# Two layer stacks on one core: resident tensors at 2048-byte addresses, feed-forward row sums ahead of the weights' low parts

## The chip, the core and the metric

The kernel runs on one core of a Trainium2 chip. A core has five engines: TensorE (PE in the profile; its weight loads are PEld), VectorE (DVE), ScalarE (ACT), GpSimd (POOL) and SyncE (SP), which issues the DMAs here. The metric is device time in microseconds. Before the change the median of three runs is 2491.5 us (2491.39 to 2491.71).

## The reference

A residual stream x of 512 tokens x 1024 features goes through two layers of a first stack and two layers of a second one, all in float32.

```
for l in range(2):                                  # first stack
    hn = rms_norm(h, g_mix[l]); q, k, v, xr, gr = split(hn @ w_in[l])
    o = differential attention(rope(q), rope(k), v); y = rg_lru(conv(xr)) * gelu(gr)
    h = h + concat(o, y) @ w_out[l]
    hm = rms_norm(h, g_mlp[l])
    h = h + square(relu(hm @ w_mlp_in[l])) @ w_mlp_out[l]
    h = h + sigmoid(rms_norm(h, g_ple[l]) @ w_ple_gate[l]) * (p[l] @ w_ple_proj[l])
x = rms_norm(h, g_final)
for l in range(2):                                  # second stack
    u, q, k, v, iq, ik, iw = split(rms_norm(x, g_pre_mix[l]) @ w_in[l])
    mix = concat(pool_mixer(u), attention(q, k, v over the top 128 keys by iq, ik, iw)) @ w_out[l]
    x = x + rms_norm(mix, g_post_mix[l])
    f = square(relu(rms_norm(x, g_pre_ffn[l]) @ w_ff1[l])) @ w_ff2[l]
    x = x + rms_norm(f, g_post_ffn[l])
```

The feed-forward width is 4096, in four blocks of 1024.

## The kernel before

Everything is kept transposed: features on the 128 partitions, the 512 tokens along the row. A float32 product is made of three passes in the fp32r format: each operand is split into a rounded high part and the low part that is left, and TensorE adds high x high, high x low and low x high (`three_passes`, its matmul is L472). The weights stream through SBUF in chunks of 128 x 2048 floats. SP loads a chunk into one half of `wr`; ScalarE rounds it into `wh` (L406) and VectorE subtracts to get `wl` (L412); TensorE reads `wh` and `wl` as the stationary operand (128 columns at a time). The moving operand is the normed stream in `gh`/`gl` or the hidden values in `hh`/`hl`. The names change places in every second stage: in stages 2 and 4 of the four the stream is in `hh`/`hl` and the hidden values in `gh`/`gl`. In the second stack a few first chunks are put where the hidden values will be, and so `gh` or `hh` is the stationary operand there.

A feed-forward layer has four blocks. In each, 4 chunks (8 tiles of 24 matmuls of 512 columns) make the hidden values, and 4 chunks add their product with the second matrix. In the first three blocks ("fast" blocks, 12 in the kernel) this second product has seven half-width products in the place of eight: GpSimd forms sums of the weights (`sum_weights`, L752 to L757), ScalarE and VectorE split each of the seven forms (L769, L781), and the hidden values need sums too. Those are made pair by pair of tiles: `rectify` (L703) takes a tile out of PSUM, ScalarE squares it (L789, L790), `even_low` (L809, L810), `other_sums` (L818 to L821), `odd_low` (L828) and `sums_low` (L835, L838) give the sums and their low parts, the last from what ScalarE rounds in L796 and L802. The matmuls of that second product have 256 columns; those on `rounded` read the sums.

Nothing is scheduled by a planner. Each engine's program is written out in order, engines are in step by semaphores, and an instruction that waits holds all that stands behind it on its engine. `fast_block_dve` is VectorE's order for a fast block. Before the even tile of pair i = 3 is through `even_low`, TensorE cannot start the fourth part of the first form; before L838 of pair 3 it cannot end the forms two to five. In the second stack VectorE waits, ahead of the first fast block, until GpSimd has zeroed the rows to which the result is added (`zeroed`, L2070).

Of the kernel before, what the change touches and what calls it, by code (L numbers as in the profile page):

```python
# [138 lines left out]
def build(nc, weights, params_a, params_b, gains, gates, embed, constants, positions, xt, out):  # L139

    with ExitStack() as ctx:
        def sb(name, shape, dtype=F32):
            return ctx.enter_context(nc.sbuf_tensor(name, shape, dtype))


        tiles = {name: sb(name, [P, KT, S], F32R) for name in ("gh", "gl", "hh", "hl")}
        with nc.sbuf_tensor("rounded", [P, ARENA], F32R) as rounded:
            pass
        arena = sb("arena", [P, ARENA])
        rest = dict(  # L150
            x=sb("x", [P, KT, S]), wr=sb("wr", [P, 2, CHUNK]), wh=sb("wh", [P, 2, CHUNK], F32R), wl=sb("wl", [P, 2, CHUNK], F32R),
            cst=sb("cst", [P, C_N]), par=sb("par", [P, max(AP_N, BP_N)]), rb=sb("rb", [P, S]), sq=sb("sq", [P, 2, S]),
            tmp=sb("tmp", [P, 4, S]), small=sb("small", [P, 256]), extra=sb("extra", [P, 7 * HALF + 2 * S]), rounded=rounded, arena=arena,
            ps=ctx.enter_context(nc.psum_tensor("ps", [P, 8, S], F32)))
# [669 lines left out]
def odd_low(dve, mem, sem, p):  # L824

    k = 2 * (p % PAIRS) + 1
    dve.wait_ge(sem["hidden_high"], 4 * p + 4)
    dve.tensor_tensor(mem.hl[:, k, :], mem.tmp[:, 3, :], mem.hh[:, k, :].bitcast(F32), ALU.subtract).then_inc(sem["hidden_low"], 1)  # L828


def sums_low(dve, mem, sem, p):

    q = p % PAIRS
    dve.wait_ge(sem["sums_high"], 2 * p + 1)
    dve.tensor_tensor(mem.hl[:, 2 * q, HALF:S], mem.tmp[:, 2, 0:HALF], mem.hh[:, 2 * q, HALF:S].bitcast(F32), ALU.subtract)  # L835
# [136 lines left out]
def fast_block_dve(dve, mem, sem, c0, j, tile_of, split_ahead, bank, target):  # L972

    for i in range(BC):
        p = PAIRS * j + i
        rectify(dve, mem, sem, tile_of[c0 + i], 2 * i, bank=bank(tile_of[c0 + i]))
        even_low(dve, mem, sem, p)
        rectify(dve, mem, sem, tile_of[c0 + i] + 1, 2 * i + 1, bank=bank(tile_of[c0 + i] + 1))
        if i < 2 and split_ahead:
            split_low(dve, mem, sem, c0 + i + 2)  # L980
        if i == 2:
            form_low(dve, mem, sem, c0 + BC, range(4))
        other_sums(dve, mem, sem, p)
# [929 lines left out]
def second_stack_layer(stage, layer, weights, params, gains, positions, out):  # L1913
# [301 lines left out]
    def program_dve(dve):  # L2215
# [650 lines left out]
```

## Time and profile before

| what | value |
|---|---|
| median of three runs | 2491.5 us |
| the profiled execution's own time | 2496.87 us |
| its span, first to last instruction | 2495.1 us |
| PE busy | 2395.5 us, 96% |
| DVE busy | 1737.2 us, 70% |
| ACT busy | 1062.2 us, 43% |
| POOL busy | 796.8 us, 32% |
| mean granted TensorE clock | 0.985 |

The span and the execution's own time are 1.8 us apart. TensorE is busy nearly all the time; matmuls are pipelined, so one's duration in a row (0.39 us) is longer than the distance from start to start (0.23 us), and it is this distance that counts. A clock of 1.00 in a window is 2.4 GHz, 0.50 is 1.2 GHz.

### The profile page before, as it was taken

What the parts mean: (1) busy time and instruction counts of PE and PEld (TensorE: products, weight loads), DVE (VectorE), ACT (ScalarE), POOL (GpSimd) and SP (SyncE); (2) the same over time, 40 slices, a digit from 0 to 9 for tenths busy, and PEclk for the clock granted to TensorE, in tenths of its full rate; (3) what the DMA queues carried; (4) which work ended last, traced back from release to release, by engine and by line L of the source; (5) the groups of instructions that cost most, each with busy time, mean ns of one, the idle gap of its engine ahead of it and who ended that gap; (6) DMA issues with size and microseconds to landing.
All of it is one profiled execution on the core that took longest, in us unless ns stands there. A gap on an engine that the chain in (4) does not pass through costs nothing.

```text
span 2495.1 us, 34122 instructions
## 1 busy us (share of the span) xinstructions
PE 2395.5 (96%) x13186; PEld 1984.8 (80%) x13186; DVE 1737.2 (70%) x2881; ACT 1062.2 (43%) x1739; POOL 796.8 (32%) x606
## 2 busy tenths in 40 slices
PE   8999999999999999999999998999999999899997
PEld 6876888988787788898876876988886777788886
DVE  6786777845778577784569857786657966777753
ACT  4554434434355443443432453444343245434431
POOL 2002344501200243450247522352312832254412
PEclk9999999999999999999999999999999999899999
DMA  4211123132231212323222120322321211132231
GB/s 155 97 65 68 68 101 119 68 118 85 100 103 59 72 68 101 119 76 111 85 89 85 55 86 34 108 79 102 119 102 56 85 51 69 51 119 98 72 119 51
DMA packets 33230, 216.23 MB, mean 87 GB/s; under 512 B 4144, under 2 KB 4400, under 8 KB 8112
## 3 DMA queue, kind: packets, MB, share of 16 engines
q1 hardware_dynamic: 33072, 214.08, 24.3%
q8 instruction: 105, 1.72, 0.3%
q14 instruction: 53, 0.43, 0.1%
HBM read 211.97 MB, written 2.10 MB: 86 GB/s over the span
## 4 chain that ended last, share of the span: by engine, by line
PE 54%; DVE 14%; issue 13%; POOL 11%; ACT 5%; DMA 3%; SPq 0%; POOLq 0%; ACTq 0%; DVEq 0%
PE ps L472 47%; DVE wl L412 4%; DMA wr<-in_weights 3%; POOL arena L752 2%; ACT wh L406 2%; DVE wl L781 2%; POOL arena L754 2%; POOL arena L945 2%; POOL arena L757 1%; POOL arena L756 1%; POOL x L945 1%; DVE tmp L703 1%; PE ps L2622 1%; PE ps L2577 1%; DVE gl L694 1%
## 5 line engine op out<-in xcount | busy, mean ns | idle before, releaser
L472 PE MATMUL ps<-gh,wh 128*128 128x512 f32 (+2 forms) x1480 | 555.1, 375 | 33.9 <-DVE gl L694 10.3
L472 PE MATMUL ps<-hh,wh 128*128 128x512 f32 (+2 forms) x1448 | 540.6, 373 | 24.7 <-DVE hl L809 9.5
L472 PE MATMUL ps<-gl,wh 128*128 128x512 f32 (+2 forms) x1480 | 544.3, 368 | 0.0
L472 PE MATMUL ps<-gh,wl 128*128 128x512 f32 (+2 forms) x1480 | 543.9, 368 | 0.0
L472 PE MATMUL ps<-hh,wl 128*128 128x512 f32 (+2 forms) x1448 | 530.5, 366 | 0.0
L472 PE MATMUL ps<-hl,wh 128*128 128x512 f32 (+2 forms) x1448 | 530.4, 366 | 0.0
L412 DVE TENSOR_TENSOR wl<-wr,wh 128x2048 fp32r<-128x2048 f32 x120 | 278.5, 2321 | 197.1 <-ACT wh L406 194.9
L472 PEld LDWEIGHTS ps<-gh,wh 128*128 128x128 f32 (+1 forms) x1480 | 281.1, 190 | 99.7 <-issue 18.3
L406 ACT ACTIVATE wh<-wr 128x2048 fp32r<-128x2048 f32 x136 | 259.5, 1909 | 211.4 <-PE ps L472 125.8
L472 PEld LDWEIGHTS ps<-hh,wh 128*128 128x128 f32 (+1 forms) x1448 | 274.1, 189 | 87.2 <-issue 21.3
L472 PEld LDWEIGHTS ps<-gh,wl 128*128 128x128 f32 (+1 forms) x1480 | 281.1, 190 | 50.8
L472 PEld LDWEIGHTS ps<-gl,wh 128*128 128x128 f32 (+1 forms) x1480 | 280.7, 190 | 48.7 <-issue 1.4
L472 PEld LDWEIGHTS ps<-hh,wl 128*128 128x128 f32 (+1 forms) x1448 | 274.5, 190 | 48.9
L472 PEld LDWEIGHTS ps<-hl,wh 128*128 128x128 f32 (+1 forms) x1448 | 274.0, 189 | 47.3 <-issue 1.4
L472 PE MATMUL ps<-rounded,wh 128*128 128x256 f32 x1152 | 212.8, 283 | 4.6 <-DVE rounded L838 3.3
L781 DVE TENSOR_TENSOR wl<-arena,wh 128x512 fp32r<-128x512 f32 x192 | 179.4, 960 | 10.3 <-ACT wh L769 10.3
L769 ACT ACTIVATE wh<-arena 128x512 fp32r<-128x512 f32 x192 | 112.6, 625 | 171.0 <-POOL arena L754 86.3
L472 PEld LDWEIGHTS ps<-rounded,wh 128*128 128x128 f32 x1152 | 177.9, 191 | 7.1 <-DVE rounded L838 4.9
L472 PE MATMUL ps<-rounded,wl 128*128 128x256 f32 x576 | 162.3, 282 | 0.0
L703 DVE SCALAR_TENSOR_TENSOR tmp<-ps,rb 128x512 f32<-128x512 f32 x128 | 87.6, 686 | 99.1 <-PE ps L472 81.0
L781 DVE TENSOR_TENSOR wl<-wr,wh 128x512 fp32r<-128x512 f32 x144 | 142.0, 994 | 20.9 <-ACT wh L769 20.9
L752 POOL TENSOR_TENSOR arena<-wr 128x512 f32<-128x512 f32 x48 | 74.1, 1544 | 235.8 <-DMA wr<-in_weights 235.8
(303 smaller groups left out, 3703.7 us busy)
## 6 DMA issues: line engine op xcount, KB each, us to landing
wr<-in_weights SPq DMA_DIRECT2D x195, 1024.0 KB, 4.7
out_yt<-x SPq DMA_DIRECT2D x8, 256.0 KB, 2.0
x<-in_xt SPq DMA_DIRECT2D x3, 512.0 KB, 8.9
wr<-in_weights SPq DMA_DIRECT2D x2, 512.0 KB, 5.8
arena<-in_gates SPq DMA_DIRECT2D x2, 512.0 KB, 8.0
arena<-in_embed SPq DMA_DIRECT2D x2, 512.0 KB, 5.6
par<-in_params_b SPq DMA_DIRECT2D x2, 274.0 KB, 2.8
x<-in_xt SPq DMA_DIRECT2D x2, 256.0 KB, 4.6
```

Source lines behind the costliest of these rows:

```text
L406: act.activation(sem.high_part(c), mem.wr[:, sem.buffer(c), :], ACT.Copy).then_inc(sem["high"], 1)
L412: dve.tensor_tensor(sem.low_part(c), mem.wr[:, sem.buffer(c), :], sem.high_part(c).bitcast(F32), ALU.subtract)\
L472: done = pe.matmul(out, stationary, moving, start=(first and n == 0), stop=(last and n == 2), skip_group_check=True)
L694: dve.scalar_tensor_tensor(out=mem.gl[:, k, :], in0=mem.x[:, k, :], scalar=gains[:, k:k + 1], in1=mem.gh[:, k, :].bitcast(F32), op0=ALU.mu ...
L703: dve.scalar_tensor_tensor(out=mem.tmp[:, k % 2, :], in0=mem.ps[:, tile % 4 if bank is None else bank, :], scalar=0.0, in1=mem.rb[:, :], o ...
L752: pool.tensor_tensor(sums[:, 0, :], raw[:, 3, :], raw[:, 2, :], ALU.add).then_inc(sem["weight_sums"], 1)
L754: pool.tensor_tensor(sums[:, 1, :], sums[:, 0, :], raw[:, 0, :], ALU.subtract).then_inc(sem["weight_sums"], 1)
L756: pool.tensor_tensor(sums[:, 2, :], raw[:, 1, :], sums[:, 1, :], ALU.subtract).then_inc(sem["weight_sums"], 1)
L757: pool.tensor_tensor(sums[:, 3, :], raw[:, 0, :], raw[:, 3, :], ALU.subtract).then_inc(sem["weight_sums"], 1)
L769: act.activation(sem.form(c, f)[0], weight_form(mem, sem, c, f), ACT.Copy) .then_inc(sem["high" if f == FORMS - 1 else "form_high"], 1)
L781: done = dve.tensor_tensor(low, weight_form(mem, sem, c, f), high.bitcast(F32), ALU.subtract)
L945: last = pool.tensor_tensor(target[row][:, part], target[row][:, part], u[:, n, :], ALU.add)
```

## The change

There are three edits.

Addresses. Tensors are laid out one after another. The first one began at 1024 + 128 = 1152 bytes of each partition, and a new tensor `margin` of 896 bytes lets it begin at 2048. `gh`, `gl`, `hh`, `hl` have 16384 bytes each, so they began at 1152 modulo 2048 and begin at 0 now. The arena has 15376 x 4 = 61504 bytes, which is 64 more than a multiple of 2048. It stood ahead of `x`, `wr`, `wh`, `wl`, so these began at 1216 modulo 2048; it now stands behind them, and they begin at 0. The arena, and `rounded` over the same bytes, began at 1152 and begin at 0 too. `cst`, `par`, `rb`, `sq`, `tmp`, `small` and `extra` come behind all of these in both kernels; `cst` began at 1216 and begins at 64.

VectorE's order in a fast block. `sums_low` is cut in two, and `first_sum_low`, `other_sums` and `odd_low` go ahead of the split of the next weights. In the first pair of a block, in the first stack (L412 is the split of a chunk, L703 the next tile), VectorE has before:

```order
L703 SCALAR_TENSOR_TENSOR tmp<-ps,rb 128x512
L412 TENSOR_TENSOR wl<-wr,wh 128x2048
L818 TENSOR_TENSOR extra<-tmp 128x256
L819 TENSOR_TENSOR extra<-tmp 128x256
L821 TENSOR_TENSOR extra<-tmp,extra 128x256
L828 TENSOR_TENSOR hl<-tmp,hh 128x512
L835 TENSOR_TENSOR hl<-tmp,hh 128x256
L838 TENSOR_TENSOR rounded<-extra,rounded 128x768
```

and now, where L824, L825, L827, L834, L841 and L849 are the old L818, L819, L821, L828, L835 and L838, L709 is L703 and L418 is L412:

```order
L709 SCALAR_TENSOR_TENSOR tmp<-ps,rb 128x512
L841 TENSOR_TENSOR hl<-tmp,hh 128x256
L824 TENSOR_TENSOR extra<-tmp 128x256
L825 TENSOR_TENSOR extra<-tmp 128x256
L827 TENSOR_TENSOR extra<-tmp,extra 128x256
L834 TENSOR_TENSOR hl<-tmp,hh 128x512
L418 TENSOR_TENSOR wl<-wr,wh 128x2048
L849 TENSOR_TENSOR rounded<-extra,rounded 128x768
```

Five instructions pass the split, and one (L835, now L841) passes four others as well. In the third pair the first four forms' lows (L781) stand where the split stood. VectorE has there before:

```order
L781 TENSOR_TENSOR wl<-wr,wh 128x512
L781 TENSOR_TENSOR wl<-arena,wh 128x512 x3
L818 TENSOR_TENSOR extra<-tmp 128x256
L819 TENSOR_TENSOR extra<-tmp 128x256
L821 TENSOR_TENSOR extra<-tmp,extra 128x256
L828 TENSOR_TENSOR hl<-tmp,hh 128x512
L835 TENSOR_TENSOR hl<-tmp,hh 128x256
```

and now, with L787 for L781:

```order
L841 TENSOR_TENSOR hl<-tmp,hh 128x256
L824 TENSOR_TENSOR extra<-tmp 128x256
L825 TENSOR_TENSOR extra<-tmp 128x256
L827 TENSOR_TENSOR extra<-tmp,extra 128x256
L834 TENSOR_TENSOR hl<-tmp,hh 128x512
L787 TENSOR_TENSOR wl<-wr,wh 128x512
L787 TENSOR_TENSOR wl<-arena,wh 128x512 x3
```

The same five pass four instructions. In the fourth pair only L835 moves. In the first fast block of a layer of the second stack pairs one and two have no split, and there, too, only L835 moves.

The wait for the zeroed rows. It stood ahead of the first `rectify` of the second stack's feed-forward layers and stands ahead of the first addition of a block now, some 45 instructions later.

```diff
@@ build
+        sb("margin", [P, (2048 - DMA_SCRATCH % 2048 - 128) // 4])
         tiles = {name: sb(name, [P, KT, S], F32R) for name in ("gh", "gl", "hh", "hl")}
-        with nc.sbuf_tensor("rounded", [P, ARENA], F32R) as rounded:
-            pass
-        arena = sb("arena", [P, ARENA])
         rest = dict(
             x=sb("x", [P, KT, S]), wr=sb("wr", [P, 2, CHUNK]), wh=sb("wh", [P, 2, CHUNK], F32R), wl=sb("wl", [P, 2, CHUNK], F32R),
+            rounded=overlaid("rounded", [P, ARENA], F32R), arena=sb("arena", [P, ARENA]),
...
-def sums_low(dve, mem, sem, p):
+def first_sum_low(dve, mem, sem, p):
     q = p % PAIRS
     dve.wait_ge(sem["sums_high"], 2 * p + 1)
     dve.tensor_tensor(mem.hl[:, 2 * q, HALF:S], ...)
+
+def other_sums_low(dve, mem, sem, p):
+    q = p % PAIRS
     dve.wait_ge(sem["sums_high"], 2 * p + 2)
     dve.wait_ge(sem["hidden_sums"], 4 * p + 3)
     dve.tensor_tensor(mem.tl[:, q, :], ...)
@@ fast_block_dve
         rectify(dve, mem, sem, tile_of[c0 + i] + 1, 2 * i + 1, bank=bank(tile_of[c0 + i] + 1))
+        first_sum_low(dve, mem, sem, p)
+        other_sums(dve, mem, sem, p)
+        if i == 3:
+            form_low(dve, mem, sem, c0 + BC, (4,))
+        odd_low(dve, mem, sem, p)
         if i < 2 and split_ahead:
             split_low(dve, mem, sem, c0 + i + 2)
         if i == 2:
             form_low(dve, mem, sem, c0 + BC, range(4))
-        other_sums(dve, mem, sem, p)
-        if i == 3:
-            form_low(dve, mem, sem, c0 + BC, (4,))
-        odd_low(dve, mem, sem, p)
-        sums_low(dve, mem, sem, p)
+        other_sums_low(dve, mem, sem, p)
     for oc in range(BC):
...
         if oc == 0:
             form_low(dve, mem, sem, c, (5, 6))
+            if sem.stage.second:
+                dve.wait_ge(sem["zeroed"], 2)
@@ second_stack_layer, program_dve
         for j in range(FAST):
-            if j == 0:
-                dve.wait_ge(sem["zeroed"], 2)
             fast_block_dve(dve, mem, sem, B_FF + 2 * BC * j, j, B_TILE, j > 0, b_bank, branch)
```

## Rows read from the trace of the kernel before

**Rows 1.** The page, part 1: busy us (share of the span) xinstructions.

```profile
PE 2395.5 (96%) x13186; PEld 1984.8 (80%) x13186; DVE 1737.2 (70%) x2881; ACT 1062.2 (43%) x1739; POOL 796.8 (32%) x606
```

**Rows 2.** Waits of PE, longest in total: us in total, times, longest us.

```profile
PE ps L472 <- DVE tmp L703: 15.9, 2, 8.0
...
PE ps L472 <- DVE gl L809: 9.9, 6, 4.2
PE ps L472 <- DVE hl L809: 9.5, 6, 4.0
...
PE ps L472 <- DVE rounded L838: 3.3, 8, 0.5
```

**Rows 3.** Chain in order of time, a wide stretch: start us, us, what.

```profile
69.01 44.81 PE ps L472 x192
```

**Rows 4.** Timeline, PE, stage 4, stationary gh: start us, us, instruction, count, [idle].

```profile
1874.48 0.39 PE L472 MATMUL ps<-hh,gh 128*128 128x512 f32 x1
...
1884.00 0.39 PE L472 MATMUL ps<-hh,gh 128*128 128x512 f32 x1
```

**Rows 5.** Timeline, PE, stage 3, stationary wh of 72 columns, first and last.

```profile
1292.71 0.39 PE L472 MATMUL ps<-gh,wh 128*72 128x512 f32 x1
...
1297.92 0.40 PE L472 MATMUL ps<-gh,wl 128*72 128x512 f32 x1
```

**Rows 6.** Timeline, PE, 256-column matmuls, two fast blocks, twelve apart each.

```profile
300.95 0.28 PE L472 MATMUL ps<-hh,wh 128*128 128x256 f32 x1
...
302.37 0.40 PE L472 MATMUL ps<-rounded,wh 128*128 128x256 f32 x2
...
381.82 0.28 PE L472 MATMUL ps<-hh,wh 128*128 128x256 f32 x1
...
383.18 0.39 PE L472 MATMUL ps<-rounded,wh 128*128 128x256 f32 x2
```

**Rows 7.** Groups by form, PE: xcount | busy us, mean ns | idle before.

```profile
L472 PE MATMUL ps<-gh,wh 128*128 128x512 f32 x1088 | 443.2, 407 | 23.7 <-DVE gl L694 10.3 <-DVE tmp L703 8.0 <-DVE extra L931 2.5
...
L472 PE MATMUL ps<-hh,wh 128*128 128x512 f32 x1056 | 427.8, 405 | 15.1 <-DVE tmp L703 8.0 <-DVE extra L931 2.5 <-DVE arena L2252 2.1
...
L472 PE MATMUL ps<-rounded,wh 128*128 128x256 f32 x1152 | 212.8, 283 | 4.6 <-DVE rounded L838 3.3 <-DVE wl L781 1.3
```

**Rows 8.** Timeline, DVE, first stack, first fast block.

```profile
254.97 2.29 DVE L412 TENSOR_TENSOR wl<-wr,wh 128x2048 fp32r<-128x2048 f32 x1 [3.03 <-ACT wh L406]
...
260.06 0.68 DVE L703 SCALAR_TENSOR_TENSOR tmp<-ps,rb 128x512 f32<-128x512 f32 x1
...
286.38 0.42 DVE L809 TENSOR_TENSOR hl<-tmp,hh 128x256 fp32r<-128x256 f32 x1 [1.00 <-ACT hh L790]
```

**Rows 9.** Timeline, PE, first fast block of stages 1 and 3.

```profile
286.86 0.58 PE L472 MATMUL ps<-hh,wh 128*128 128x256 f32 x1 [3.98 <-DVE hl L809]
...
1560.81 0.39 PE L472 MATMUL ps<-hh,wh 128*128 128x256 f32 x1 [3.14 <-DVE hl L809]
```

**Rows 10.** Windows: us, busy of PE, PEld, DVE, ACT, POOL, PEclk, DMA share, GB/s.

```profile
285.20:292.00 6.80, 5.14 (x24) 5.14 (x25) 5.10 (x12) 5.46 (x11) 0.00 (x0) 0.50 0.00 1
...
1561.80:1565.20 3.40, 3.40 (x18) 3.40 (x17) 2.82 (x7) 3.29 (x6) 0.00 (x0) 0.50 0.00 0
```

**Rows 11.** Timeline, ACT, stage 3, ahead of the first rectify.

```profile
1529.20 0.60 ACT L683 ACTIVATE rb<-ps 128x512 f32<-128x512 f32 x1 [5.41 <-PE ps L346]
```

**Rows 12.** Timeline, POOL, the same stretch.

```profile
1525.20 3.56 POOL L2070 MEMSET arena<- 128x3072 f32 x2
...
1534.21 1.48 POOL L752 TENSOR_TENSOR arena<-wr 128x512 f32<-128x512 f32 x1
```

**Rows 13.** Timeline, DVE, the same stretch.

```profile
1529.84 0.69 DVE L703 SCALAR_TENSOR_TENSOR tmp<-ps,rb 128x512 f32<-128x512 f32 x1 [2.25 <-ACT rb L683]
...
1535.83 1.49 DVE L818 TENSOR_TENSOR extra<-tmp 128x256 f32<-128x256 f32 x1 [0.70 <-ACT tmp L789]
...
1540.65 0.41 DVE L835 TENSOR_TENSOR hl<-tmp,hh 128x256 fp32r<-128x256 f32 x1
```

More of the change, by code:

```diff
@@ L100 @@
 PI_BELOW = 3.1415925
+DMA_SCRATCH = 1024
 class Steps:
@@ L143, in sb, with overlaid @@
             return ctx.enter_context(nc.sbuf_tensor(name, shape, dtype))
+        def overlaid(name, shape, dtype):
+            with nc.sbuf_tensor(name, shape, dtype) as place:
+                return place
+        sb("margin", [P, (2048 - DMA_SCRATCH % 2048 - 128) // 4])
         tiles = {name: sb(name, [P, KT, S], F32R) for name in ("gh", "gl", "hh", "hl")}
-        with nc.sbuf_tensor("rounded", [P, ARENA], F32R) as rounded:
-            pass
-        arena = sb("arena", [P, ARENA])
         rest = dict(
             x=sb("x", [P, KT, S]), wr=sb("wr", [P, 2, CHUNK]), wh=sb("wh", [P, 2, CHUNK], F32R), wl=sb("wl", [P, 2, CHUNK], F32R),
+            rounded=overlaid("rounded", [P, ARENA], F32R), arena=sb("arena", [P, ARENA]),
             cst=sb("cst", [P, C_N]), par=sb("par", [P, max(AP_N, BP_N)]), rb=sb("rb", [P, S]), sq=sb("sq", [P, 2, S]),
-            tmp=sb("tmp", [P, 4, S]), small=sb("small", [P, 256]), extra=sb("extra", [P, 7 * HALF + 2 * S]), rounded=rounded, arena=arena,
+            tmp=sb("tmp", [P, 4, S]), small=sb("small", [P, 256]), extra=sb("extra", [P, 7 * HALF + 2 * S]),
             ps=ctx.enter_context(nc.psum_tensor("ps", [P, 8, S], F32)))
@@ L2857 @@
     from concourse.bass_utils import run_bass_kernel_spmd
-    nc = bacc.Bacc("TRN2", target_bir_lowering=False, num_devices=1, dynamic_dma_scratch_size=1024)
+    nc = bacc.Bacc("TRN2", target_bir_lowering=False, num_devices=1, dynamic_dma_scratch_size=DMA_SCRATCH)
     arrays = {f"in_{name}": a for name, a in launch_arrays(inputs).items()}
```

## The prediction

> **What bounds the kernel now.** I read the page's first part, then TensorE's waits, then the distance between its matmuls. TensorE is busy for 96% of the span [rows 1], so time can come from two places alone: its waits, and the pace of its matmuls. The list of its waits is short [rows 2]. Two waits of 8.0 us are for `rectify` (L703), 12 waits of 19.4 us in all are for `even_low` (L809), and 8 of 3.3 us for the row sums' lows (L838). The reader is to see that all of these are VectorE's work in the fast blocks.
>
> The pace is the other place. In a stretch of wide matmuls with the stationary operand in `wh` or `wl`, 192 of them take 44.81 us, which is 0.2334 us each [rows 3]. In stage 4 the first chunks lie in `gh`, and there the same kind of matmul goes 42 times in 9.52 us, 0.2267 us each [rows 4]. In stage 3 a stationary operand of 72 columns in `wh` gives 5.21 us over 23, 0.2265 us [rows 5]. So 0.0067 us of each wide matmul depends on the stationary operand. `gh` starts at the same place modulo 2048 as the moving `hh`; `wh` starts 64 bytes off it. The narrow matmuls have two paces, 1.42 us or 1.36 us for twelve, 0.118 or 0.113 each [rows 6], with the same operands in the same places; which of the two holds in a block is not settled by the address.
>
> **The change part by part.** The profiled execution took 2496.87 us, 1.8 more than its span of 2495.1, and 5.4 more than the median of 2491.5. I take the sum off the profiled time and then off the median.
>
> *VectorE's order, first stack, first fast block of a layer (2).* VectorE stands idle 3.03 us for ScalarE's L406 before the first split, and reaches the next `rectify` at 260.06 [rows 8]. The split lasts until 257.26 whatever stands around it. Behind it stood L818 to L838; now L838 alone does, 0.9 us, so that `rectify` can start at about 258.1, 2.0 us earlier. The five that moved need 0.4 to 0.7 us each, 2.3 us in all, and fit in the 3.03 us, as ScalarE's squares that they wait for come ahead of L406 on its queue. The second pair is the same, and the third gives 1 us more in front of L781. Together that is 5 us by the time of L809 of pair four, which ends at 286.80 and for which TensorE waits 3.98 us [rows 8, 9]; its twin in stage 2 is 4.2 [rows 2]. Both waits go: 8.2 us. From 285.20 to 292.00, right behind that wait, the granted clock is 0.50, 1.2 GHz in place of 2.4, and 24 matmuls run there [rows 10]. With 24 starts in 5.1 us (286.86 to 292.0) they are 0.213 us apart in place of 0.118: 2.3 us lost. I count 1.5 us for the shorter stretch in stage 2. Sum 12. Late next is L838 of pair four, by my count 0.5 us ahead of its use.
>
> *Second stack, first fast block (2).* Pairs one and two have no split to pass. The 8.0 us wait stays: L818 begins at 1535.83 and takes 1.49 us [rows 13] beside GpSimd's weight sums (L752, [rows 12]), where others of its kind take 0.41 (L835 [rows 13]), and so do the two behind it. L835 now goes first. It costs nothing where it fits in the 0.70 us that VectorE idles before L818 [rows 13], and 1.08 us where it too is held; L838 waits for ScalarE behind L821 anyway. I take 0, bounds -0.4 and +1.1. Pair three gives 1.3 us, of which I count 1.0, off a wait of 3.14 [rows 9]. It is followed by 3.4 us at clock 0.50 with 18 matmuls [rows 10], about 1.5 us lost; with a wait of 2 us instead I give that an even chance. Sum 2 x 1.0 + 1.5 = 3.5.
>
> *The other eight fast blocks.* Of the 19.4 us for L809, 2 x 4.1 and 2 x 3.1 are used up; 5.0 remain, plus 3.3 for L838, and each of the 16 stops costs some 0.15 us until the pace is regained: 10.7. VectorE gains 2 us on the first pair, but is then at TensorE's pace; in pair three the sums now run beside GpSimd's second set of weight sums, and 1.08 us more for each of four would take 4 of what is won. I still find the next `rectify` 0.9 us earlier, more than the 0.6 needed. I take 9.5, bounds 0 and 10.7.
>
> A rule speaks against this. [rows 13] show a VectorE instruction with two SBUF inputs at 1.49 us beside GpSimd and 0.41 us alone. The Trainium skill (SBUF — State Buffer, "Who interferes with whom") says that such an instruction and a GpSimd one that reads SBUF exclude each other, and that the second to issue fully blocks. By this rule, the trace agrees, each instruction moved under GpSimd's sums pays one of them; that is the 4 us above.
>
> *The wait for zeroed rows.* GpSimd's two memsets begin at 1525.20 and have 3.56 us [rows 12], so they end at 1528.76. The first `rectify` starts at 1529.84, released by ScalarE's L683, which ends at 1529.80 [rows 11, 13]. The memsets were 1.0 us early: the move gives 0. Behind the new wait stands the first addition, by then 30 us later: 0. Bounds 0 and 0.1.
>
> Order in all: 12 + 3.5 + 9.5 = 25 us; bounds 8 and 30.
>
> *Addresses.* The wide matmuls with `wh` or `wl` number 3 x 1088 + 3 x 1056 = 6432 [rows 7], as each group of three passes has one such row. Now stationary and moving operands both begin at 0 modulo 2048, the relation that `gh` and `hh` had in rows 4. At 0.0067 us each that is 42.9 us. Some is given back. In the eight later fast blocks the hidden values' 192 matmuls end 1.3 us sooner while VectorE's chain does not, and I put 0.7 us of new wait there: 5.6. At norms and in attention VectorE or ScalarE end some waits: 3. This leaves 34. The narrow matmuls of the fast blocks are 12 blocks x 4 chunks x 7 forms x 4 parts x 3 passes = 4032, of which 1152 are the row on `rounded` and `wh` [rows 7]. With half of them at either pace of rows 6, all could come to 0.113, 2016 x 0.0045 = 9 us, or all to 0.118, 9 us the other way; as place decides nothing in rows 6 I take less than half of the gain. I take -4. VectorE and ScalarE should not change: their durations differ by GpSimd, not by where a tensor lies. Addresses in all: 38 us; bounds 0, by rows 6 where place decides nothing, and 52; below zero see the rivals.
>
> Sum: 25 + 38 = 63 us. 2496.9 - 63 = 2433.9 for a profiled execution, 2491.5 - 63 = 2428.5 for the median; I say 2429.
>
> **The rivals.**
>
> *The pace does not follow the address.* Rows 4 and 5 may differ from rows 3 by something else: a stationary operand of 72 columns in `wh`, 64 bytes off, was as fast as the one in `gh`. Narrow matmuls also change pace in one place. Then order alone counts: 2491.5 - 25 = 2466.5. The rows in favour are 5 and 6, against are rows 3 and 4, where place is all that I can find to differ. The Trainium skill (SBUF — State Buffer, "Who interferes with whom") gives TensorE two independent read ports, one for the moving operand and one for weight loads, and says that it never waits on anyone; TensorE: Matmul & The Clock Gate, "Back-to-back issue gap", has 512/2.4 + 2.5 = 215.8 ns for a start-to-start distance, an estimate by that page. By these, no address could matter; the trace has 0.2334 and 0.2267 us and so departs from the figure in both cases.
>
> *The order gives little as GpSimd takes it back.* The four sums in pair three, each 1.08 us longer, and L835 in the second stack cost 4 us per block. Then only the first stack's 12 us remain, minus 2 x 1.1: some 10. With the pace it is 2444, without it 2482.
>
> *Slower: operands in step.* Both streams now start at 0 modulo 2048, every one of them, where 64 bytes kept `wh` off before. If weight loads and the moving stream then meet at the same place, each wide matmul loses another 0.0067 us, the step between the two paces seen, 43 us, and the narrow ones all stay at 0.118, 9 us. Minus 25 for the order that is 2491.5 + 52 - 25 = 2518.5. It decides from 0.004 us per wide matmul on. Against it stand rows 4: there the two begin at the same place modulo 2048 and run at the better pace, at 1152 rather than 0.
>
> **How the numbers follow.** Forecast (both gains) 0.50; pace unchanged 0.30 (2466.5); order largely taken back 0.11 (2444 or 2482, half each); in step 0.06 (2518.5); 0.03 for something better than 2412. The likeliest case's own range is 2412 to 2446. For 8 in 10 I leave out the slow case and half of the weakest one, and the bounds of the order term go to both sides: 2414 to 2477. A difference of 0.2%, 5 us, is what a measurement of this kernel can tell from none. Faster by more: 0.50 + 0.30 + 0.11 + 0.03, less 0.08 for doubts about the bounds of the order term, 0.86; slower 0.08; within 0.2% 0.06.
>
> **What would show it.** In TensorE's waits the row on L809 should fall from 19.4 us to about 5, L838 to under 2, and the 15.9 us for L703 should stay. The clock should hold at 1.00 where rows 10 have 0.50 in stage 1. A wide stretch of 192 should take 43.5 us where rows 3 have 44.81; if it is 44.8 the first rival holds, if it is 46 the last. VectorE's idle time of 3.03 us before L412 should fall to under 1 us. I am wrong if the pace changes by another amount than 0.0067 us, if it changes in some stretches alone, or if new waits for L809 appear in the eight later blocks.

## The result, and the profile after

The changed kernel takes 2470.15 us (median of 4 runs, 2469.1 to 2471.06), the kernel before 2491.61 beside it: ratio 0.9913, 95% interval 0.9896 to 0.993. That is 21.4 us less. Forecast were 62.5 us less (2429). The time lies in the range of 2414 to 2477, but a third of the forecast gain came.

Line numbers move by 6 to 14: L472 is L478 now, L412 is L418, L703 L709, L809 L815, L818 to L821 are L824 to L827, L828 L834, L835 L841, L838 L849, L781 L787, L752 to L757 L758 to L763, L2070 L2084. The kernels of the experiments have them a few lines off: L478, L709 and L815 are L479, L710 and L816 in `place_only`, and L478 and L815 are L474 and L811 in `order_only`.

The first part of the page after (columns as in [rows 1]):

```profile
PE 2364.6 (96%) x13186; PEld 1997.2 (81%) x13186; DVE 1793.7 (73%) x2881; ACT 1058.3 (43%) x1739; POOL 787.9 (32%) x606
```

TensorE's share is unchanged, while VectorE, with the same 2881 instructions, is busy for 56 us more. The prediction had a part of that, four times 1.08 us in each of eight blocks, 34.6 us. It comes with the order: VectorE is busy for 1739.1 us with the new places alone and for 1781.5 with the new order alone. TensorE's waits after, as in [rows 2]:

```profile
PE ps L478 <- DVE tmp L709: 16.2, 2, 8.1
PE ps L478 <- DVE hl L815: 15.0, 6, 4.1
PE ps L478 <- DVE gl L815: 14.3, 6, 4.1
```

The waits for `even_low` rose from 19.4 to 29.3 us, where about 5 were forecast. Those of 3.3 us for the row sums' lows are gone, and the two long ones for `rectify` stand where they stood. The pace is the other half. The chain after has the stretch of [rows 3] as

```profile
67.02 43.58 PE ps L478 x192
```

which is 0.2270 us per wide matmul. The narrow ones, PE's timeline as in [rows 6], twelve starts from the first row here to the last:

```profile
295.37 0.40 PE L478 MATMUL ps<-rounded,wh 128*128 128x256 f32 x2
...
296.81 0.28 PE L478 MATMUL ps<-hh,wh 128*128 128x256 f32 x1
```

1.44 us for twelve, 0.120 each, slower than either pace of [rows 6]. Over the whole trace, the distances between successive starts that nothing interrupts give this ledger (TensorE's records, before to after):

| part | before | after | difference |
|---|---|---|---|
| wide on `wh` or `wl`, uninterrupted | 1434.6 us, 233.3 ns each (6149) | 1400.8, 227.3 ns (6164) | -33.8 |
| the same, with a wait or at the lower clock | 127.0 | 121.4 | -5.6 |
| narrow (256 columns), uninterrupted | 537.7, 116.3 ns (4624) | 553.5, 119.9 ns (4615) | +15.8 |
| narrow, with a wait or at the lower clock | 73.6 | 72.8 | -0.8 |
| all others | 298.8 | 295.5 | -3.3 |

Together -27.7 us, where the two spans (2495.1 and 2467.3) differ by 27.8. The medians differ by 21.4, as the profiled execution of before lay 5.4 above its median and that of the changed kernel 1.0 below.

Now the stretch on which the order term rested, VectorE in pair two of the first fast block (timeline: start us, us, instruction, [idle before and what ended it]):

```profile
256.63 0.68 DVE L709 SCALAR_TENSOR_TENSOR tmp<-ps,rb 128x512 f32<-128x512 f32 x1
257.24 0.42 DVE L841 TENSOR_TENSOR hl<-tmp,hh 128x256 fp32r<-128x256 f32 x1
258.02 0.43 DVE L824 TENSOR_TENSOR extra<-tmp 128x256 f32<-128x256 f32 x1 [0.37 <-ACT tmp L795]
258.36 0.42 DVE L825 TENSOR_TENSOR extra<-tmp 128x256 f32<-128x256 f32 x1
258.69 1.53 DVE L827 TENSOR_TENSOR extra<-tmp,extra 128x256 f32<-128x256 f32 x1
260.14 1.78 DVE L834 TENSOR_TENSOR hl<-tmp,hh 128x512 fp32r<-128x512 f32 x1
261.85 3.37 DVE L418 TENSOR_TENSOR wl<-wr,wh 128x2048 fp32r<-128x2048 f32 x1
265.14 2.04 DVE L849 TENSOR_TENSOR rounded<-extra,rounded 128x768 fp32r<-128x768 f32 x1
267.11 0.68 DVE L709 SCALAR_TENSOR_TENSOR tmp<-ps,rb 128x512 f32<-128x512 f32 x1
```

and GpSimd beside it:

```profile
258.46 1.48 POOL L758 TENSOR_TENSOR arena<-wr 128x512 f32<-128x512 f32 x1 [18.97 <-DMA wr<-in_weights]
260.02 1.36 POOL L760 TENSOR_TENSOR arena<-arena,wr 128x512 f32<-128x512 f32 x1
261.45 1.62 POOL L762 TENSOR_TENSOR arena<-wr,arena 128x512 f32<-128x512 f32 x1
263.03 3.34 POOL L763 TENSOR_TENSOR arena<-wr 128x512 f32<-128x512 f32 x1
```

The reader is to see that from 258.69 on each VectorE instruction takes about 1.1 us more than elsewhere (L827 1.53 instead of 0.42, L834 1.78 instead of 0.69, L418 3.37 instead of 2.29, L849 2.04 instead of 0.95), one for each of GpSimd's four weight sums: 4.4 us. The idle time of 3.04 us before the split in this pair is gone, as forecast, but the next `rectify` comes no sooner. The same stretch with the old order is in `place_only` below.

### The profile page after: what moved, and what is told of

Its sections match the earlier page's. It is cut to its first block, busy times and chain, and to the rows that moved or that the text cites. A ratio compares the mean times of both kernels' runs of the same rounds, so it can differ in the third digit from the quotient of the medians.

```text
span 2467.3 us, 34122 instructions
## 1 busy us (share of the span) xinstructions
PE 2364.6 (96%) x13186; PEld 1997.2 (81%) x13186; DVE 1793.7 (73%) x2881; ACT 1058.3 (43%) x1739; POOL 787.9 (32%) x606
## 4 chain that ended last, share of the span: by engine, by line
PE 71%; DVE 20%; ACT 4%; issue 2%; POOL 1%; DMA 0%; POOLq 0%; SPq 0%; DVEq 0%; ACTq 0%
PE ps L478 64%; DVE wl L418 2%; DVE wl L787 2%; DVE extra L827 1%; DVE tmp L709 1%; ACT tmp L795 1%; DVE rounded L849 1%; DVE arena L2321 1%; PE ps L2634 1%; DVE extra L824 1%; PE ps L2589 1%; DVE extra L825 1%; DVE small L2316 1%; PE ps L2667 1%; DVE gl L700 1%
## 5 line engine op out<-in xcount | busy, mean ns | idle before, releaser
L478 PE MATMUL ps<-gh,wh 128*128 128x512 f32 (+2 forms) x1480 | 550.4, 372 | 35.8 <-DVE gl L815 14.3
L478 PE MATMUL ps<-hh,wh 128*128 128x512 f32 (+2 forms) x1448 | 535.8, 370 | 28.6 <-DVE hl L815 15.0
L478 PE MATMUL ps<-gh,wl 128*128 128x512 f32 (+2 forms) x1480 | 539.8, 365 | 0.0
L478 PE MATMUL ps<-gl,wh 128*128 128x512 f32 (+2 forms) x1480 | 539.5, 365 | 0.0
L478 PE MATMUL ps<-hh,wl 128*128 128x512 f32 (+2 forms) x1448 | 526.2, 363 | 0.0
L478 PE MATMUL ps<-hl,wh 128*128 128x512 f32 (+2 forms) x1448 | 526.1, 363 | 0.0
L418 DVE TENSOR_TENSOR wl<-wr,wh 128x2048 fp32r<-128x2048 f32 x120 | 279.0, 2325 | 141.2 <-ACT wh L412 138.9
L478 PEld LDWEIGHTS ps<-gh,wh 128*128 128x128 f32 (+1 forms) x1480 | 282.1, 191 | 93.8 <-issue 18.9
L412 ACT ACTIVATE wh<-wr 128x2048 fp32r<-128x2048 f32 x136 | 259.5, 1909 | 204.4 <-PE ps L478 120.1
L478 PEld LDWEIGHTS ps<-hh,wh 128*128 128x128 f32 (+1 forms) x1448 | 275.6, 190 | 82.7 <-issue 20.7
L478 PEld LDWEIGHTS ps<-gh,wl 128*128 128x128 f32 (+1 forms) x1480 | 281.8, 190 | 44.6
L478 PEld LDWEIGHTS ps<-gl,wh 128*128 128x128 f32 (+1 forms) x1480 | 282.2, 191 | 42.7 <-issue 1.4
L478 PEld LDWEIGHTS ps<-hh,wl 128*128 128x128 f32 (+1 forms) x1448 | 275.5, 190 | 42.9
L478 PEld LDWEIGHTS ps<-hl,wh 128*128 128x128 f32 (+1 forms) x1448 | 275.8, 190 | 41.3 <-issue 1.4
L478 PE MATMUL ps<-rounded,wh 128*128 128x256 f32 x1152 | 220.2, 288 | 0.0
L787 DVE TENSOR_TENSOR wl<-arena,wh 128x512 fp32r<-128x512 f32 x192 | 189.2, 1010 | 2.5 <-ACT wh L775 2.5
L478 PEld LDWEIGHTS ps<-rounded,wh 128*128 128x128 f32 x1152 | 184.4, 197 | 0.6
L478 PE MATMUL ps<-rounded,wl 128*128 128x256 f32 x576 | 165.7, 288 | 0.0
L709 DVE SCALAR_TENSOR_TENSOR tmp<-ps,rb 128x512 f32<-128x512 f32 x128 | 87.6, 685 | 105.8 <-PE ps L478 88.1
L758 POOL TENSOR_TENSOR arena<-wr 128x512 f32<-128x512 f32 x48 | 75.2, 1567 | 267.5 <-DMA wr<-in_weights 267.5
L795 ACT ACTIVATE tmp<-tmp 128x512 f32<-128x512 f32 x96 | 60.6, 632 | 223.3 <-DVE tmp L709 223.3
```

The source lines that it names most:

```text
L412: act.activation(sem.high_part(c), mem.wr[:, sem.buffer(c), :], ACT.Copy).then_inc(sem["high"], 1)
L418: dve.tensor_tensor(sem.low_part(c), mem.wr[:, sem.buffer(c), :], sem.high_part(c).bitcast(F32), ALU.subtract)\
L478: done = pe.matmul(out, stationary, moving, start=(first and n == 0), stop=(last and n == 2), skip_group_check=True)
L758: pool.tensor_tensor(sums[:, 0, :], raw[:, 3, :], raw[:, 2, :], ALU.add).then_inc(sem["weight_sums"], 1)
L787: done = dve.tensor_tensor(low, weight_form(mem, sem, c, f), high.bitcast(F32), ALU.subtract)
L795: act.activation(value, source, ACT.Square).then_inc(sem["hidden_high"], 1)
```

## The experiments

**Places and order apart.** `place_only` is the kernel before with the new allocation; `order_only` is the changed kernel with the old one.

```diff
+        sb("margin", [P, (2048 - DMA_SCRATCH % 2048 - 128) // 4])
...
-        arena = sb("arena", [P, ARENA])
...
+            rounded=overlaid("rounded", [P, ARENA], F32R), arena=sb("arena", [P, ARENA]),
```

That is `place_only` against before; `order_only` has the same lines the other way, against the changed kernel.

> The tensors' new places with the old order of VectorE and the old wait for zeroed rows. Theory A (pace: wide matmuls 0.2334 to 0.2267 us, 6432 of them, -43 us; narrow matmuls of 256 columns to 0.120 us, some +19 us; the order gives next to nothing because VectorE's moved sums meet GpSimd's): -20 us or a little more, 2468 to 2472, all of what the whole change gives, narrow matmuls at 0.120. Rival B (the order is worth its 25 us of the prediction, and places are worth almost nothing net): 2488 to 2493. Rival C (the order costs time, since VectorE's busy time rose by 56 us): places alone give more than the whole change, 2455 to 2466.

> The new order and the moved wait, with every tensor where it lay before. Theory A: within 5 us of before, 2487 to 2495; the wide pace stays at 0.2334, the first split of a fast block waits under 1 us for ScalarE in place of 3.03, but VectorE's sums and lows of pair two and three take 1.5 to 1.8 us each beside GpSimd, and the waits for even_low stay near 4 us in first fast blocks. Rival B: 2466 to 2472, as forecast for the order alone. Rival C: 2496 or more.

`place_only`: 2471.01 us (5 runs), ratio 0.9916, interval 0.9903 to 0.993. `order_only`: 2488.34, 0.998, 0.9971 to 0.9989. The places alone give all that the whole change gives, 21 to 22 us; the order alone gives 4.6, and nothing visible on top of the places. Theory A held; B and C fell. What the 4.6 us are isn't shown. The two kernels have the same places, but the narrow matmuls are not equally fast in them: 116.3 ns from start to start in the trace of before, 115.3 in `order_only` (worked out from TensorE's records), and 1.0 ns times 4800 is 4.8 us. Of the twelve fast blocks four run at about 114 and eight at about 117 ns in the one, eight and four in the other. The runs of `order_only` also spread more, from 2483.5 to 2492.5 (11 runs). The waits for `even_low` of the two (PE's waits):

```profile
PE ps L479 <- DVE hl L816: 14.4, 6, 5.0
PE ps L479 <- DVE gl L816: 14.1, 6, 4.8
```

```profile
PE ps L474 <- DVE gl L811: 11.2, 6, 3.4
PE ps L474 <- DVE hl L811: 10.4, 6, 3.4
```

So the places alone raise these waits from 19.4 to 28.5 us, as TensorE reaches them sooner, and with the order alone they are 21.6, also more than before. VectorE's old order in pair two, `place_only`:

```profile
259.50 0.68 DVE L710 SCALAR_TENSOR_TENSOR tmp<-ps,rb 128x512 f32<-128x512 f32 x1
263.21 2.49 DVE L419 TENSOR_TENSOR wl<-wr,wh 128x2048 fp32r<-128x2048 f32 x1 [3.02 <-ACT wh L413]
265.62 1.51 DVE L825 TENSOR_TENSOR extra<-tmp 128x256 f32<-128x256 f32 x1
267.06 0.41 DVE L826 TENSOR_TENSOR extra<-tmp 128x256 f32<-128x256 f32 x1
```

```profile
259.51 1.30 POOL L759 TENSOR_TENSOR arena<-wr 128x512 f32<-128x512 f32 x1 [19.12 <-DMA wr<-in_weights]
260.88 1.29 POOL L761 TENSOR_TENSOR arena<-arena,wr 128x512 f32<-128x512 f32 x1
262.26 1.29 POOL L763 TENSOR_TENSOR arena<-wr,arena 128x512 f32<-128x512 f32 x1
263.51 3.34 POOL L764 TENSOR_TENSOR arena<-wr 128x512 f32<-128x512 f32 x1
```

Here is where the forecast's gain was. In the old order VectorE stands idle for 3.02 us from 260.2 to 263.2, and GpSimd makes most of its sums in exactly that time; of the four only the third costs VectorE 0.2 us (L419, 2.49) and the fourth 1.1 (L825, 1.51). The idle time that the new order fills was not free: it was GpSimd's turn. Between the first `rectify` of one pair and that of the next (worked out from VectorE's timeline):

| first fast block, stage 1 | pair 1 to 2 | 2 to 3 | 3 to 4 | sum |
|---|---|---|---|---|
| before | 11.18 | 12.46 | 12.17 | 35.8 |
| `place_only` | 11.18 | 12.47 | 12.28 | 35.9 |
| changed | 9.16 | 12.85 | 13.04 | 35.1 |
| `first_pair_early` | 9.17 | 13.96 | 11.68 | 34.8 |
| `quiet_old` | 11.18 | 11.17 | 10.09 | 32.4 |
| `quiet_new` | 9.17 | 9.15 | 9.37 | 27.7 |
| `dve_sums_one` | 9.17 | 11.82 | 12.26 | 33.2 |
| `dve_sums_two` | 9.16 | 11.81 | 11.30 | 32.3 |
| `dve_two_old` | 11.17 | 13.82 | 12.73 | 37.7 |

**Without GpSimd's sums.** Both kernels with the new places, GpSimd's weight sums cut to 32 of 512 columns. Most of the sums is left out, so what these two kernels compute is not the result; they serve for the time alone.

```diff
-    pool.tensor_tensor(sums[:, 0, :], raw[:, 3, :], raw[:, 2, :], ALU.add).then_inc(sem["weight_sums"], 1)
+    pool.tensor_tensor(sums[:, 0, 0:32], raw[:, 3, 0:32], raw[:, 2, 0:32], ALU.add).then_inc(sem["weight_sums"], 1)
```

The other three sums are cut in the same way.

> The changed kernel with GpSimd's weight sums of the fast blocks cut to 32 of 512 columns each (the rest of the sums is left out, so part of the weights' forms is stale), which makes GpSimd's 4 instructions per set short. Theory (the order gains nothing because VectorE's moved sums meet GpSimd's): now the first fast block's pairs two and three go at about 9 to 11 us like pair one and the order gives what was forecast: even_low waits 29.3 us fall to under 6, with the clock held behind them; 2440 to 2450. Rival F (the order's gain is limited by ScalarE or by TensorE's own pace, not by GpSimd): 2460 to 2472.

> The same cut of GpSimd's weight sums, with the new places and the old order. Theory: without GpSimd the old order still waits for ScalarE's split behind which the sums stand, so it is 6 to 15 us slower than quiet_new: 2452 to 2462. Rival F: no difference from quiet_new.

`quiet_new`: 2421.35 us (4 runs), ratio 0.9715, 0.9698 to 0.9731. `quiet_old`: 2433.04 (4 runs), 0.9764, 0.9748 to 0.978. The order is now worth 11.7 us, and the first block's three distances are 7.4 us shorter than changed ones; F fell. Pair two takes 9.15 us, and its instructions have their short durations back:

```profile
259.43 0.48 DVE L827 TENSOR_TENSOR extra<-tmp,extra 128x256 f32<-128x256 f32 x1
259.83 0.74 DVE L834 TENSOR_TENSOR hl<-tmp,hh 128x512 fp32r<-128x512 f32 x1
261.08 2.29 DVE L418 TENSOR_TENSOR wl<-wr,wh 128x2048 fp32r<-128x2048 f32 x1 [0.51 <-ACT wh L412]
```

Both came about 20 us lower than expected: with their sums GpSimd costs this kernel 49 us (2470.15 to 2421.35), far more than I had read off the `even_low` waits. Part of it is a wait that I had taken as fixed: in `quiet_new` TensorE waits

```profile
PE ps L478 <- DVE tmp L709: 5.6, 2, 2.8
PE ps L478 <- DVE gl L815: 2.8, 1, 2.8
PE ps L478 <- DVE hl L815: 2.8, 1, 2.8
```

The two waits of 8.1 us for `rectify` in the second stack fell to 2.8 each, and ten of the twelve for `even_low` are not there any more: 34.3 us of the 49. TensorE's mean granted clock rose with it, from 0.987 to 0.993 in the profiled executions. The 11.7 us are still less than the 25 of the forecast; with the sums cut, the old order has only 12.6 us of `even_low` waits left to lose.

**The new order in the first pair only**, of the changed kernel.

```diff
 ...
+        if i in (0,):
+            first_sum_low(dve, mem, sem, p)
+            other_sums(dve, mem, sem, p)
+            odd_low(dve, mem, sem, p)
 ...
+        if i not in (0,):
+            other_sums(dve, mem, sem, p)
 ...
```

> The changed kernel, but VectorE's new order only in the first pair of a fast block; pairs two to four have the old order (sums behind the split or the forms' lows). Theory (pair one has no GpSimd beside it and gains 2.0 us; pairs two and three lose 0.4 and 0.9 us to GpSimd's weight sums): even_low waits of the first fast blocks in stages 1 and 2 fall from 4.13 to about 3 us, those of the eight later blocks from 2.0 to 1.4, in all 5 to 8 us less waiting, with some 1 us back for the rounded lows: 2463 to 2468. Rival (the new order helps in every pair): as place_only at best, with waits of 4.8 to 5.0 in the first blocks, 2471 or more.

2467.91 us (4 runs), ratio 0.9901, 0.9884 to 0.9918, within the expected 2463 to 2468 but inside the changed kernel's interval. The waits for `even_low` are 25.1 us instead of 29.3. The expected 3 us in the first blocks of stages 1 and 2 was a miss (3.9 and 3.7): with pair two 2 us earlier, GpSimd's set, whose start is set by the weights' arrival, falls on other instructions of it (13.96 us in the table). What is won in one pair is in part lost in the next.

**VectorE makes the sums.** If four sums on GpSimd hold VectorE up for 4.4 us and VectorE needs 0.69 for a sum of this size, it should make them itself, in a kernel that computes everything.

```diff
         other_sums_low(dve, mem, sem, p)
+        if i == 1:
+            sum_weights(dve, mem, sem, c0 + BC)
+        if i == 2:
+            sum_weights(dve, mem, sem, c0 + BC + 1)
 ...
-    sum_weights(pool, mem, sem, c0 + BC)
```

The second `if` is in `dve_sums_two` alone, and there GpSimd's call for that set is taken out too; `dve_two_old` has the same on `place_only`. `sum_weights` also waits for the four sums of the set before it. GpSimd keeps the rest.

> The changed kernel, computing everything, but the first of the four sets of weight sums in each fast block is made by VectorE at the end of pair two (4 subtractions of 128x512, about 2.7 us by the same size elsewhere on VectorE) and no longer by GpSimd. Theory (what takes back the order's gain is GpSimd's sums standing beside VectorE's two-input work, 4.3 us per set): pair two to three falls from 12.85 and 13.65 us to about 12, pair three to four stays at 13.04; even_low waits fall by 0.9 to 1.6 us in each of 10 blocks: 2456 to 2463. Rival (VectorE's own load decides, whoever runs beside it): pair two to three rises by 2.7 us, 2470 to 2490.

> As dve_sums_one, and the second set too, by VectorE at the end of pair three. Theory: pair three to four falls from 13.04 to about 12.1 as well; even_low waits under 12 us in all; 2446 to 2458. Rival: each set costs VectorE 2.7 us more than it frees, 2475 to 2510.

> dve_sums_two with VectorE's old order (the new places stay): sums behind the split or the forms' lows, two sets of weight sums on VectorE, two on GpSimd. Theory (the order's gain was hidden by GpSimd's sums alone): now the order shows, so this kernel is 7 to 13 us slower than dve_sums_two at 2446.7, as the two kernels with cut sums were 11.7 apart: 2453 to 2460. Rival (the order gives nothing once VectorE carries the sums): 2444 to 2450.

`dve_sums_one`: 2453.43 us (5 runs), 0.9837, 0.9824 to 0.985, 2.6 us below what was expected, as pair three gained too: GpSimd's remaining set starts at 268.17 there, 3.2 us earlier than in the changed kernel. `dve_sums_two`: 2446.66 (5 runs), 0.9815, 0.9801 to 0.9828, better than either kernel. VectorE's sums in it (`sum_weights` is L760 to L765 here, `even_low` L817, in `dve_two_old` L818):

```profile
263.00 0.68 DVE L760 TENSOR_TENSOR arena<-wr 128x512 f32<-128x512 f32 x1
263.72 0.69 DVE L762 TENSOR_TENSOR arena<-arena,wr 128x512 f32<-128x512 f32 x1
264.44 0.69 DVE L764 TENSOR_TENSOR arena<-wr,arena 128x512 f32<-128x512 f32 x1
265.06 0.69 DVE L765 TENSOR_TENSOR arena<-wr 128x512 f32<-128x512 f32 x1
265.66 0.68 DVE L709 SCALAR_TENSOR_TENSOR tmp<-ps,rb 128x512 f32<-128x512 f32 x1
```

2.7 us for the four, on an engine that has 96 instructions more and is busy for 34.6 us less (1759.1 to 1793.7). Its waits of TensorE, and those with the old order:

```profile
PE ps L478 <- DVE gl L817: 7.4, 2, 6.0
PE ps L478 <- DVE hl L817: 6.8, 2, 5.5
PE ps L478 <- DVE tmp L709: 5.4, 2, 2.7
```

```profile
PE ps L479 <- DVE hl L818: 30.2, 6, 8.0
PE ps L479 <- DVE gl L818: 30.2, 6, 8.0
```

The waits for `even_low` are 14.2 us, where under 12 were expected, most of it in the second stack (5.5 and 6.0); the two for `rectify` fell from 16.2 to 5.4 us, which no expectation had. Together these waits are 25.9 us less than in the changed kernel, for 23.5 us less time.

`dve_two_old` takes 2502.86 us (5 runs), 1.0042, 1.0029 to 1.0056: slower than before, and 56 us behind `dve_sums_two`. Theory and rival had 7 to 13 us and none; the sign of the theory held, its size missed by far. The old order leaves VectorE idle for 3.02 us in pairs one and two and then does the sums as well, so that pair two takes 13.82 us and TensorE waits 60.4 us in all for `even_low`, 46.2 more than in `dve_sums_two`. The mean granted clock is 0.980 against 0.989 in the profiled executions; that this makes up the rest of the 56 us was not worked out. The value of the order, set beside what GpSimd does:

| | old order | new order | order |
|---|---|---|---|
| old places | 2492.9 | 2488.3 | -4.6 (cause not shown, see above) |
| new places | 2471.0 | 2470.2 | -0.8 (not told from 0) |
| new places, sums cut | 2433.0 | 2421.4 | -11.7 |
| new places, two sets on VectorE | 2502.9 | 2446.7 | -56.2 |

**Which places count.**

```diff
-            x=sb("x", [P, KT, S]), wr=sb("wr", [P, 2, CHUNK]), ...
+            x=sb("x", [P, KT, S]), pad_wr=sb("pad_wr", [P, 16]), wr=sb("wr", [P, 2, CHUNK]), ...
```

This is `w_off_64`. `w_off_128` and `w_off_32` have pads of 32 and 8 words; `rounded_64` has 16 words ahead of `rounded` and `arena` instead; `base_1152` is without the margin, `base_64` has one of 960 bytes, and `places_mixed` has pads of several sizes.

> The changed kernel with 64 bytes of padding ahead of wr, so that wr, wh, wl and the scratch begin at 64 modulo 2048, and gh, gl, hh, hl and x stay at 0. Theory A1 (the pace goes by the distance between stationary and moving operand): wide matmuls with wh or wl go back to 0.233 us and those on wh with hidden halves to 0.113 to 0.118, about 2487 to 2492; sums' matmuls (rounded, now at 64 like wh) tell apart whether it is the distance to the moving operand (0.120) or wh's own place (0.113 to 0.118). Rival D (the pace goes by where the moving tensors begin, 1152 against 0): all stays as changed, 2468 to 2472.

> The changed kernel without the margin: all resident tensors begin at 1152 modulo 2048, equal to each other. Theory A1 (distance counts): 2468 to 2473, wide 0.2267, narrow 0.120. Rival D (multiples of 2048 count): wide back to 0.233, 2487 to 2492.

> The changed kernel with 64 bytes of padding ahead of the scratch, so that the hidden row sums (rounded) lie 64 bytes off the weights' forms and everything else stays. Theory A1 (each matmul's pace goes by the distance of its own two operands; wide ones want 0, narrow ones want 64): the 1728 narrow matmuls on rounded go from 0.120 to 0.115 us, the 2304 narrow ones on hidden halves stay at 0.120, wide ones stay at 0.2267: 8 to 9 us less than the changed kernel, 2461 to 2463. Rival E (narrow matmuls need wh itself off a multiple of 128): nothing changes, 2470.

> The changed kernel with all resident tensors at 64 modulo 2048 instead of 0. If only the distance counts: wide 0.2267, narrow 0.120, 2468 to 2473. If the place modulo 128 counts too: another pace in one of them.

> The changed kernel with many distances in one: gh and wh at 0, gl at 32, hh at 128, hl at 256, wl at 64, the scratch at 512 (modulo 2048). By the theory of distances each pass then has its own pace: wide gh,wh at 0.2267, those with a distance of 64 at 0.233 as before; which of 32, 128, 256, 512 behaves like 0 is not known. If only 64 modulo 128 is special, 128, 256 and 512 all run like 0 (0.2267 wide, 0.120 narrow).

> The changed kernel with 128 bytes of padding ahead of wr: wr, wh, wl and the scratch at 128 modulo 2048, so hh and gh stand 128 off wh. If 64 modulo 128 is what costs wide matmuls: as changed, wide 0.2267, narrow 0.120. If any distance but 0 modulo 2048 costs: wide 0.230 to 0.236, narrow under 0.120.

> The same with 32 bytes. If the pace follows the distance gradually: wide between 0.2267 and 0.2334, narrow between 0.115 and 0.120. If the unit is 64 bytes: like the changed kernel.

Time, and uninterrupted distance between starts in ns, of the wide matmuls `gh,wh`, the narrow `hh,wh` and the narrow `rounded,wh` (TensorE's records, averages). In brackets the bytes, modulo 2048, of the weights' operands above the moving `gh` and `hh`, and above the moving `rounded`. Those with one run are single executions.

| kernel | us | wide | narrow hidden | narrow rounded |
|---|---|---|---|---|
| before (64, 64) | 2492.9 | 233.3 | 116.6 | 116.0 |
| `order_only` (64, 64) | 2488.3 | 233.4 | 114.8 | 114.8 |
| changed (0, 0) | 2470.2 | 227.3 | 119.8 | 119.9 |
| `base_1152` (0, 0), 4 runs | 2472.0 | 227.3 | 119.9 | 119.9 |
| `base_64` (0, 0), one run | 2468.9 | 227.5 | 119.8 | 119.9 |
| `w_off_64` (64, 0), 10 runs | 2488.5 | 233.3 | 115.0 | 118.0 |
| `rounded_64` (0, -64), 4 runs | 2468.3 | 227.1 | 120.0 | 118.0 |
| `w_off_128` (128, 0), one run | 2486.6 | 232.7 | 119.0 | 118.7 |
| `w_off_32` (32, 0), one run | 2486.9 | 233.2 | 118.0 | 119.2 |

`w_off_64` differs from the changed kernel by 64 bytes alone and is back at the time of `order_only`; its chain has the stretch of 192 as

```profile
66.88 44.82 PE ps L479 x192
```

`base_1152` and `base_64` show that beginning at a multiple of 2048 does nothing by itself: what the fast kernels share is that stationary and moving tensors begin at the same place modulo 2048. No run tells whether 256 or 512 would do in the place of 2048. Distances of 32, 64 and 128 all cost a wide matmul 5 to 6 ns (rival D fell, and so did the thought that a unit of 64 bytes or a multiple of 128 is as good as none). For the narrow ones it is the other way round: equal places are the worst measured, 120 ns, though 128 bytes (119.0) is hardly better. `rounded_64` was expected at 2461 to 2463 and gave 2468.3, about 2 us less than the changed kernel and hardly told from it: its matmuls on `rounded` went to 118, not to 115. `places_mixed`, with gl at 32, hh at 128, hl at 256, wl at 64 and the scratch at 512, took 2480.9 in one run, and it contradicts a rule by one pair's distance. Its wide `gh,wh`, at distance 0, take 232, 233 or 236 ns and not 227; its `hh,wh`, 128 bytes apart, mostly 224, where `w_off_128` has 232.7. So the places of the other matmuls of a sequence matter too; how, no run shows. What gives both 227 and 113 wasn't found.

## Why the prediction was wrong

The two steps that failed are the order's gain in the pairs of a fast block, and the pace of the narrow matmuls. That 2470 lies in the range is luck: it is near the first rival's 2466.5, which had nothing from the places and 25 us from the order, and the runs show the reverse.

*Wide pace: right.* Forecast 6432 x 6.7 ns, put as 42.9 us (it is 43.1); measured 233.3 to 227.3, 6.0 ns, 38.6 us. The first rival (pace doesn't follow place) and the last (in step is slower) fell for these. The stationary operands of 72 columns in `wh` don't follow: they were fast 64 bytes off [rows 5], and at equal places they are slower, 232.1 ns on average against 227.3 before (45 distances of TensorE's records each). So [rows 5] was no evidence for the step of 0.0067 us, and why 72 columns behave otherwise is open.

*Narrow pace: wrong in sign, and outside its bounds.* The prediction said "as place decides nothing in rows 6" and took -4, at most 9 either way. [rows 6] had shown two paces with the same places, and I took them for the only two. The third, 120 ns, needed another place, which no row of before had. 4800 x 3.6 ns = 17 us lost (116.3 to 119.9); the 4800 are the 4032 of the fast blocks and 768 others of 256 columns, which the prediction left out. (Its step between the two paces of [rows 6] is 0.005 us, not 0.0045, so its bound of 9 is 10.) The last rival had the right idea, a loss when the operands are in step, and put most of it at the wide matmuls, which gained. Address term: 38 forecast, 21 to 22 measured (`place_only`). The "given back" was of the right kind: the waits for `even_low` rose by 9.1 us with the places alone, 5.6 had been put down. At norms 1.7 us were given back (L694 and then L700, 11.3 to 13.0 us), in attention none (L1749 and then L1763, 10.1 both times), where 3 were counted.

*Order: wrong, and the larger error.* 25 forecast, 4.6 measured without the new places (of which the narrow pace may be all), about 0 with them. The step that failed is "The second pair is the same, and the third gives 1 us more": pair one gave its 2.0 us (11.18 to 9.16), pair two lost 0.39 and pair three 0.87, so 0.8 us stood where 5 were counted, and the wait of 3.98 [rows 9] was 4.13 with a faster TensorE. The clock went with it. Windows of the stretches behind the waits of stages 1, 2 and 3, and behind a wait of 2.0 us in stage 1's second fast block, as in [rows 10]:

```profile
281.20:288.00 6.80, 5.69 (x26) 5.70 (x27) 5.81 (x12) 5.67 (x12) 0.00 (x0) 0.51 0.00 1
898.80:905.60 6.80, 6.67 (x43) 6.67 (x44) 5.76 (x12) 5.29 (x10) 0.00 (x0) 0.75 0.00 0
1544.20:1547.60 3.40, 3.40 (x17) 3.40 (x18) 3.04 (x8) 2.93 (x6) 0.00 (x0) 0.50 0.00 0
458.70:462.10 3.40, 3.40 (x19) 3.40 (x18) 3.04 (x6) 3.28 (x7) 0.00 (x0) 0.51 0.02 5
```

So neither of the first stack's stretches at 1.2 GHz went away (in stage 2 half of the 6.8 us is at 0.50, as before), and new ones came: behind four of the eight waits of 2.0 us in the later fast blocks the clock is 0.51 or 0.52 for 3.4 us (from 458.8, 987.8, 1632.9 and 2233.7 on), where it stayed at 1.00 behind the waits of 0.5 to 1.0 us before. The text had the mechanism: it counted 1.08 us for each sum beside GpSimd, but for four sums of pair three in the eight later blocks only. It did not lay GpSimd's set over pair two, where splits and lows of any size pay the same 1.1 us, and it booked the idle time before pair two's split as free, as that of pair one [rows 8] was, beside which GpSimd has no sums. Rival two, "the order gives little as GpSimd takes it back", was nearest, at a chance of 0.11. It still kept 10 us of the first stack, which did not come either, and its 2444 stood on the address term of 38.

The Trainium skill (SBUF — State Buffer, "Who interferes with whom") has VectorE's instructions with two SBUF inputs and GpSimd's that read SBUF exclude each other. The trace agrees, with up to 1.1 us for each; the rule should have been laid over the timeline of both engines, pair by pair. The same section has TensorE's two read ports independent of each other; the runs don't bear out that its pace is free of where the operands lie (227.3 or 233.3 ns by 64 bytes alone).

*Second stack, first fast block: right in pair three, wrong in the clock.* Pair three gave 1.4 us (10.09 to 8.64; 1.3 forecast), pair one 0.03 lost; in stage 3 the wait went from 3.14 to 2.94 only, in stage 4 from 2.94 to 2.03, as TensorE came sooner. The even chance for the clock was lost in stage 3 (third window above); in stage 4 no stretch at 0.50 stands behind that wait any more.

*Eight later blocks: wrong.* Forecast 0.9 us earlier, measured about 0.2 later (38.6 to 38.9 us from pair one to four): the first pair gives 2.2 us, and pairs two and three lose 1.2 and 1.3. The waits are 2.0 us each where 0.6 stood, but with the places alone they are already 1.3 to 1.6. The 3.3 us for the row sums' lows did go. The 0.15 us for each stop is rather 0.1: in the trace of before the start after the first matmul behind a stop comes after 0.222 us in place of 0.118.

*Zeroed rows: right.* GpSimd's memsets after, and the first `rectify`:

```profile
1509.94 3.56 POOL L2084 MEMSET arena<- 128x3072 f32 x2
```

```profile
1514.51 0.69 DVE L709 SCALAR_TENSOR_TENSOR tmp<-ps,rb 128x512 f32<-128x512 f32 x1 [2.19 <-ACT rb L689]
```

The memsets end at 1513.50, ScalarE still releases: 0.

## What to carry to other kernels

Before an idle gap of an engine is booked as free, look at what the other engines do in that gap, and whether their instructions lengthen each other: the gap may be what lets one of them run undisturbed. Work that is cheap on a helper engine is dear if each of its instructions holds up the main one; here 2.7 us of sums on VectorE replaced 4.4 us of standing behind GpSimd, and the new order paid clearly only after that. Where an operand's place sets the pace of matmuls, price each width by itself and measure the new place once, since the paces that a trace shows are those of its own places.

## What the runs showed of the hardware

Moving all resident tensors together, to 0, 1152 or 64 modulo 2048, changes nothing (2470.2, 2472.0 and, in one run, 2468.9 us). The distance between stationary and moving operand does, for stationary operands of 128 columns and with one distance for all: 227.3 ns at 0 and 232.7 to 233.4 at 32, 64 and 128 for 512 columns; 119.9 at 0, 115 to 117 at 64 for 256 columns on the hidden halves. With all operands 64 bytes apart (before and `order_only`) a fast block's narrow matmuls go at about 114 or at about 117 ns. A VectorE instruction with two SBUF inputs pays up to 1.1 us for meeting a GpSimd sum, less where it starts late in one (2.49 in place of 2.29), whether it takes 0.42 or 2.29 us by itself, while `rectify`, which reads PSUM, keeps its 0.68 or 0.69 in all 128 cases. GpSimd is held up in turn (L763 3.34 us against 1.3 to 1.7).
